# A gather stream spread over a second stage: the context's expert rows beside the main stream's first mixing

## The chip, the cores and the metric

The kernel runs on one core of one Trainium2 chip. The metric is the device time of one execution in microseconds (us), the median of three runs. Everything is in float32.

## The reference, cut to what matters

Two blocks run one after the other on 256 tokens of width 1024. The first has two layers of a hybrid mixer and a gated feed-forward. The second has two layers too, and a second input beside `x`, the context (256 tokens), which the second block alone uses:

```python
def reference(x, ..., ctx_2, ...):
    x = first_block(x, ...)                 # 2 x (state-space scan + retention + feed-forward)
    for l in range(2):                      # second_block
        h, hc = modulate(x, ...), modulate(ctx, ...)
        if l == 0: mix_c, kv_c = token_mix(hc)         # the context's own mixing
        else:      kv_c = keys_values(hc)
        mix_x = token_mix(h, kv_c)                     # the main stream's mixing
        x = x + m2 * mix_x
        x = x + m5 * peer(modulate(x), ...)            # experts
        if l == 0:
            ctx = ctx + m2c * mix_c
            ctx = ctx + m5c * peer(modulate(ctx), ...)
    return rmsnorm(x, final_g)

def peer(h):      # per token: 8 heads x 16 chosen experts = 128 rows of 1024
    act  = gate * gelu(sum(peer_down[e] * h))
    return sum_k act[k] * peer_up[e[k]]
```

The context's second state is read only by the keys and values of the second block's layer 1. So the context's experts are free to run anywhere between the context's own mixing and that point.

## The kernel before, in words

One program holds five engine programs. `Plan` writes one list of items (`put(kind, ...)`), and each engine walks through that list in order and does its share of each item. So the order of the list is the order of work on every engine, and an instruction that waits holds everything behind it on its engine.

Two generators write the list. `x_stream` is the main stream: the first block (two layers), then for l = 0 and 1 the mixing (`mix_phase`, with `mixer` inside) and the experts (`peer_x`). `context_stream` is the context: modulation, its mixing, and its experts (`peer_c`). `streams` interleaves them. Each `yield` adds a number of units to its stream's counter (7 where nothing is given), and the context gets a turn while its counter is at most `pace` times the main stream's. `("pace", p)` sets a new pace and aligns the counters, and `"alone"` writes all that is left of the context at once.

`PACES` is (0.8, 1.8, 1.1, 0.72): the last one is set when the context's routing is over and its expert rows begin. There are 512 such rows, in the order 128 `down` for the first 128 tokens, 128 `up` for them, then the same for the other 128 tokens. Each row is one indirect gather of 128 x 1024 floats (0.5 MB) issued by GpSimd (L2556), up to nine ahead in a ring of nine buffers, and one VectorE instruction: L2234 for `down` (multiply and reduce), L2245 for `up` (multiply and accumulate; it waits on the accumulate before it). Each row yields 1.5 units. The rows have no TensorE work. `peer_add` closes: SyncE loads a 0.5 MB row (L2627) once the last gathered row is read, and VectorE adds the result to the context (L2264, L2267).

In the list of the kernel before, the rows begin 1088 units before the end of the first block: 233 units of the feed-forward of layer 0 (22 `ffn_in`, 8 `ffn_out` and the last steps), 625 of layer 1's two mixers, and 230 of layer 1's feed-forward. The state-space scan is the first 248 units of those 625. At 0.72 they take 768 / 0.72 = 1067 units, so they end 20 units before the first block does, and `"alone"` finds nothing left.

The main stream's first mixing is 321 units: 34 for the normalisation, the low-rank projections and the keys and values, 28 for four steps of the query projection (`q_up`, with a rotation on VectorE at L2057 to L2061), 203 for attention with the gates, Fourier and pooling between its steps (`beside`), 28 for `mix` and 28 for `token_out`. An attention step gives VectorE a maximum (L2090), a scale, and, after ScalarE's exponential, a reciprocal (L2094); the transpose of that step on TensorE waits for the exponential. Of the 13 intervals between the third and the last of the 16 score steps, seven have one gate step (one weight chunk on TensorE) in between and six have none. All scratch of this mixing lies in the 27648 words from A0, except its twelve gate buffers (6144 words), which lie at B0 where the context has its memory, and which wait for the end of the context (`self.c_ok`).

Of the kernel before, what the change touches and what calls it, by code (L numbers as in the profile page):

```python
# [125 lines left out]
        self.before, self.ss, self.var, self.done = before, ss, var, done  # L126


PACES = (0.8, 1.8, 1.1, 0.72)
A_SIZE = 27648  # L130
BIG_N = 53208
SIDE = 8300
# [2 lines left out]
class Plan:  # L135
# [80 lines left out]
    def order(self):  # L216
# [7 lines left out]
        self.xmark = ar.at  # L224
        self.streams(self.x_stream(ar), self.context_stream(), PACES[0])
        self.put("finished", stored=(self.sem("d_out"), self.counts["d_out"]))
# [30 lines left out]

    def x_stream(self, ar):
        yield from self.first_block()
        yield "alone"  # L260
        for l in range(2):
            ar.at = self.xmark
            yield from self.mix_phase(self.px, Ring(self.wx), self.small, ar, l, self.X, 0, True)
            side = Arena(self.big, BIG_N - SIDE, SIDE)
            yield from self.peer_x(self.px, self.small, self.A0 + self.xmark, BIG_N - self.A0 - self.xmark - SIDE, l,
                                   self.X, iter(()) if l else self.context_keys(),
                                   [side.get(2048) for _ in range(3 if l else 4)], side if l else None)

    def context_stream(self):
# [5 lines left out]
        self.put("context_in")  # L275
        yield "pace", PACES[1]
        yield from self.mix_phase(self.pb, Ring(few), self.smallb, ar, 0, self.C, 1, False)
        yield "pace", PACES[2]
        yield from self.peer_c(self.pb, Ring(few), self.smallb, self.B0 + mark, BIG_N - self.B0 - mark, 9, 0, self.C)
# [592 lines left out]
    def mixer(self, banks, wr, sm, ar, l, hT, hT_ok, X, vec, rope_on, cs):  # L872
# [7 lines left out]
        wide = rope_on  # L880
# [3 lines left out]

        if early:
            zfT, AB, fT, zp, poT, pyT = mixed_buffers()
        if wide:
            far = ar if l else Arena(self.big, self.B0, BIG_N - self.B0)
            sg_slots = [Slot(far.get(512, (2, 256))) for _ in range(12)]
            for s in sg_slots:  # L890
                s.freed = self.c_ok
        mark = ar.at
        def spectral():
            w, u = self.load(wr, t["wzf"][l], 2048), banks.take()
            w.free(u.full)
            w2, ua = self.load(wr, t["dft"], 2048), [banks.take() for _ in range(2)]
            uf = banks.take()
            w2.free(uf.full)
            put("fourier", ws=[w, w2], u=u, ua=ua, uf=uf, hT=hT, zfT=zfT, AB=AB, fT=fT)
            got["f_ok"] = uf.free  # L900
            yield
            w, u = self.load(wr, t["wzp"][l], 2048), banks.take()
            w.free(u.full)
            w2, up = self.load(wr, t["pool"], 2048), banks.take()
            w2.free(up.full)
            w3, ug = self.load(wr, t["wgrp"][l], 256), banks.take()
            w3.free(ug.full)
            put("pool", ws=[w, w2, w3], u=u, up=up, ug=ug, hT=hT, zp=zp, poT=poT, pyT=pyT, psc=self.col[l, "psc"])
            got["py_ok"] = ug.free
            yield  # L910
# [34 lines left out]
        kv_ok = yield from kv  # L945
        if rope_on and l == 1:
            kv_ok += self.ctx_kv_ok
        low = self.low_turn(banks, sm, 256, cqn, cqT, self.col[l, "qg"], low["scaled"])
        put("low_turn_out", **low)
        turned = low["parts"][1].free  # L950
# [4 lines left out]
        for h in range(0, 8, 2):  # L955
            u = banks.take()
            q_ok = tick("q_turned") if rope_on else u.free
            put("q_up", ws=[w] if h == 0 else [], w_ok=w.full, wq=wq, cqT=cqT, Q=Q[:, h:h + 2, :], h=h, u=u, ready=turned,
                u2=banks.take() if rope_on else None, cs=cs, rt=rt, done=q_ok)
            yield  # L960
        w.free(u.full)

        nk = 4 if rope_on else 2

# [35 lines left out]
            yield from self.beside(fill, 11, attend(), 18)  # L1000
        else:
            yield from attend()
        if not wide or l == 0:
            ar.at = mark
        if not wide:
            if not early:
                zfT, AB, fT, zp, poT, pyT = mixed_buffers()
                yield from spectral()
            sg_slots = [Slot(ar.get(512, (2, 256))) for _ in range(3)]
# [34 lines left out]

    def routing(self, ar, b2, wr, sm, l, vec, hT, hT_ok, keys, keys_ok, iot, iot_ok, tvs, gat, eix, qts, GH):


        put, tick, t = self.put, self.tick, self.t
        SC0 = Ring([Slot(ar.get(256, (2, 128))) for _ in range(3 if GH == 8 else 8)])
        SC1 = ar.get(2048, (8, 256))  # L1050
# [18 lines left out]
        def gates(tt, g):  # L1069
            g3 = gat[:, tt, 16 * GH * g:16 * GH * g + 16 * GH].rearrange("p (h k) -> p h k", h=GH)  # L1070
            tv, c = tvs[tt][:, GH * g:GH * g + GH, :], sm[:, 32:32 + GH]
            exp = tick("gates_exp")
# [28 lines left out]
        def ranks(asking=None):  # L1101
            for tt in range(2):
                for h in range(8):
# [3 lines left out]
                    yield from rank(tt, h, by2(SC1[:, h, :]) if tt else sc.ap, ok, None if tt else sc)  # L1107
                    if (h + 1) % GH == 0:
                        yield from gates(tt, h // GH)

# [32 lines left out]
    def peer_c(self, banks, wr, sm, start, size, gslots, l, X):  # L1143

        put, tick, t = self.put, self.tick, self.t
        got = yield from self.peer_queries(banks, sm, start, size, l, X, 1, self.c_ok, 2)
        ar, mark, h2, act, gat, eix, gl, hT, hT_ok, keys, rest = got
        m3 = ar.at
        rows = self.modulated_rows(l, 1, 3, "norm2", h2, [ar.get(1024) for _ in range(3)], self.b_free)
        rows_ok = yield from rows(hT_ok)  # L1150
        ar.at = m3
        qts = Ring([Slot(ar.get(512, (2, 256)))])
        qts.slots[0].freed = rows_ok
        tvs = [ar.get(128, (8, 16)) for _ in range(2)]
        route, _, _, _, ix_ok, gates_ok, _ = self.routing(ar, banks, wr, sm, l, 1, hT, hT_ok, tvs=tvs, gat=gat, eix=eix, qts=qts,
                                                       GH=8, **rest)
        yield from route()
        yield "pace", PACES[3]
        ar.at = mark
        rr = Ring([Slot(ar.get(1024), self.sem(f"row{i}")) for i in range(gslots)])  # L1160
        steps = [(kind, tt, k) for tt in range(2) for kind in range(2) for k in range(128)]
        pending, ahead, nxt, act_ok = [], [], 0, {}
        acc_ok = {}
        for n, (kind, tt, k) in enumerate(steps):
            while nxt < len(steps) and len(ahead) < gslots:
                kind2, tt2, k2 = steps[nxt]
                s = rr.take()
                put("fetch", table=t["pboth"].rearrange("e (a d) -> (e a) d", a=2), s=s, index=eix[kind2][:, tt2, k2:k2 + 1],
                    ready=ix_ok[tt2][k2 // 16] if k2 % 16 == 0 else None, before=s.before or gates_ok[1, 0])
                ahead.append(s)  # L1170
                nxt += 1
            s = ahead.pop(0)
            done = tick("rows_read")
            s.free(done)
            if kind == 0:
                put("down", row=s.ap, full=s.full, h=h2[:, tt, :], out=act[:, tt, k:k + 1], done=done)
                if k == 127:
                    tanh = tick("gelu_tanh_c")
                    put("gelu_all", at=act[:, tt, :], u=gl, cubed=tick("gelu_cubed_c"), tanh=tanh)
                    act_ok[tt] = tick("act_done_c")  # L1180
                    put("gelu_all_end", at=act[:, tt, :], u=gl, gat=gat[:, tt, :], tanh=tanh, done=act_ok[tt])
            else:
                put("up", s=s, by=act[:, tt, k:k + 1], at=h2[:, tt, :], first=(k == 0), ready=act_ok[tt],
                    chain=acc_ok.get(tt), done=done)
                acc_ok[tt] = done
            yield 1.5
        end = tick("peer_added")
        put("peer_add", m5=rr.slots[0].ap, src=self.mods[l, 1, 5:6, :].to_broadcast([P, 1024]), loaded=tick("d_m5_c", 16),
            before=[done], acc=h2, X=X, done=end)
        self.c_ok, self.b_free = end, [end]  # L1190

    def peer_x(self, banks, sm, start, size, l, X, side, spare, last):
# [3 lines left out]
        wr = Ring(self.wx[:3])  # L1196
# [3 lines left out]
        ar, mark, h2, act, gat, eix, gl, hT, hT_ok, keys, rest = got  # L1200
        eix = eix[0]
        ag = ar.get(32)
        both = ar.get(1024)
        qts = Ring([Slot(both[:, 512 * i:512 * i + 512].rearrange("p (a n) -> p a n", a=2)) for i in range(2)])
        tvs = [ar.get(128, (8, 16)) for _ in range(2)]
        parts = self.routing(ar, Banks(banks.banks[4:6]), wr, sm, l, 0, hT, hT_ok, tvs=tvs, gat=gat, eix=[eix], qts=qts, GH=1, **rest)
        _, query, score, ranks, ix_ok, gates_ok, ended = parts
# [1 line left out]
        dgs = Ring([Slot(ar.get(128)) for _ in range(5)])  # L1209
        places = [ar.get(2048) for _ in range((ar.size - ar.at) // 2048)]  # L1210
        rows = self.modulated_rows(l, 0, 3, "norm2", h2, [places[-2][:, 0:1024], places[-2][:, 1024:2048], places[-1][:, 0:1024]],
                                   [self.x_ok])

        def ask():
            for i in range(8):
# [6 lines left out]
        route = ranks(asking)  # L1222
# [89 lines left out]
        for n, (tt, k) in enumerate(steps):  # L1312
            fetch_ahead()
            s, slot, _ = ahead.pop(0)
# [1482 lines left out]
```

## Time and profile before

| | |
|---|---|
| median of three runs | 4146.09 us (4141.56 to 4146.14) |
| span of the profiled execution | 4145.5 us |
| TensorE busy | 3651.7 us, 88% |
| VectorE busy | 2321.9 us, 56% |
| GpSimd busy | 1280.9 us, 31% |
| ScalarE busy | 657.1 us, 16% |
| mean granted TensorE clock | 0.955 |
| the context's 512 gathers | 1045.0 to 2131.1 us |
| the main stream's first mixing | 2182 to 2450 us |

Matmuls are pipelined and their ends are modelled, so a busy TensorE isn't one at its peak. The granted clock tells which part of full speed the array was given: 1.0 is the 2.4 GHz level, and a stretch that fell to the 1.2 GHz level for a part of its time shows a mean between 0.5 and 1.0.

### The profile page before, as it was taken

To read this page: it belongs to the slowest core of one execution; us is meant where nothing else is said; L and a number is where in the kernel's file an instruction comes from. 1 tells how busy PE (TensorE), PEld (TensorE's weight loads), DVE (VectorE), ACT (ScalarE), POOL (GpSimd) and SP (SyncE) were. 2 spreads that over 40 slices of the span, in tenths; PEclk is the share of its full clock that TensorE was granted. 3 is DMA by queue.
4 is the path that set the end of the run, shared out by engine and by line. 5 is a ranking of instruction groups with operands and counts; after the bars stand their busy time and mean duration, and the time that the engine had idled before them with its cause. 6 is when DMAs were issued, how large, how long until landed. Compare 5 with 4: busy or idle time off the path is not lost. (4 is left out here: it accounts for less than half of the span.)

```text
span 4145.5 us, 41044 instructions
## 1 busy us (share of the span) xinstructions
PE 3651.7 (88%) x14584; PEld 2584.5 (62%) x14584; DVE 2321.9 (56%) x5464; ACT 657.1 (16%) x1800; POOL 1280.9 (31%) x1125
## 2 busy tenths in 40 slices
PE   8988999999989889999988989778788898877777
PEld 6666788887756778888846875333335686433332
DVE  3432011457676897775762137787763226777875
ACT  2332101110001230000002211111112211111111
POOL 1100000000664566664540003445441002444442
PEclk9999999999999899999999999999999999998899
DMA  8742344334998889998973349999996227999997
GB/s 324 283 194 88 117 151 180 134 111 145 369 411 292 295 330 395 405 389 340 413 298 125 108 152 384 415 416 401 419 415 256 103 107 288 404 420 420 418 420 331
DMA packets 207818, 1208.65 MB, mean 292 GB/s; under 512 B 23696, under 2 KB 24848, under 8 KB 96000
## 3 DMA queue, kind: packets, MB, share of 16 engines
q0 software_dynamic: 154368, 855.71, 51.5%
q1 hardware_dynamic: 53248, 350.32, 22.2%
q8 instruction: 118, 1.93, 0.2%
q14 instruction: 84, 0.69, 0.0%
HBM read 1204.79 MB, written 1.15 MB: 291 GB/s over the span
## 5 line engine op out<-in xcount | busy, mean ns | idle before, releaser
L1363 PE MATMUL bank<-big 128*128 128x256 f32 (+5 forms) x9848 | 2148.4, 378 | 59.5 <-issue 8.7
L1363 PEld LDWEIGHTS bank<-big 128*128 128x128 f32 (+2 forms) x9848 | 1839.0, 192 | 374.3 <-issue 67.4
L2556 POOL DMA_INDIRECT big<-in_pboth,big x1024 | 1217.5, 1189 | 1210.0 <-PE bank L1750 695.2
L1750 PE MATMUL bank<-big 128*128 128x512 f32 x2048 | 984.3, 638 | 251.2 <-ACT big L2520 251.0
L2234 DVE CUSTOM_DVE_ANT_0 big<-big 128x1024 f32<-128x1024 f32 x768 | 928.0, 1224 | 347.1 <-DMA big<-in_pboth,big 343.0
L1750 PEld LDWEIGHTS bank<-big 128*128 128x128 f32 x2048 | 407.5, 204 | 816.6 <-issue 481.4
L2543 POOL TENSOR_TENSOR big<-big 128x1 f32<-128x1 f32 (+1 forms) x49 | 37.4, 763 | 1499.4 <-DVE big L1804 1499.4
L2245 DVE SCALAR_TENSOR_TENSOR big<-big 128x1024 f32<-128x1024 f32 x254 | 326.2, 1284 | 61.3 <-DMA big<-in_pboth,big 41.5
L2520 ACT ACTIVATE big<-big 128x128 f32<-128x128 f32 x512 | 165.1, 391 | 254.9 <-DVE big L2213 248.2
L1398 PE MATMUL bank<-big 128*128 128x128 f32 x596 | 93.0, 290 | 63.5 <-ACT big L2365 20.1
L2510 ACT ACTIVATE big<-big 128x4 f32<-128x4 f32 (+2 forms) x134 | 27.7, 207 | 742.3 <-DVE big L2209 742.2
L1553 PE MATMUL bank<-big 128*128 128x512 f32 x256 | 114.5, 609 | 23.4 <-DVE big L1968 23.4
L2090 DVE TENSOR_REDUCE big<-bank 128x1 f32<-128x512 f32 (+1 forms) x48 | 28.9, 602 | 175.0 <-PE bank L1651 174.1
L1398 PEld LDWEIGHTS bank<-big 128*128 128x128 f32 x596 | 72.9, 151 | 80.8 <-issue 35.2
L1877 DVE SCALAR_TENSOR_TENSOR big<-big,bank 128x512 f32<-128x512 f32 x32 | 22.0, 687 | 148.8 <-ACT big L2346 148.8
L1553 PEld LDWEIGHTS bank<-big 128*128 128x128 f32 x256 | 49.8, 195 | 87.2 <-issue 63.1
L1954 DVE SCALAR_TENSOR_TENSOR big<-big,bank 128x256 f32<-128x256 f32 x32 | 13.4, 420 | 153.4 <-PE bank L1363 153.3
L1861 DVE SCALAR_TENSOR_TENSOR big<-bank,big 128x255 f32<-128x255 f32 (+1 forms) x144 | 62.7, 477 | 60.0 <-ACT big L2334 58.3
L2303 ACT ACTIVATE big<-big 128x1024 f32<-128x1024 f32 x26 | 27.4, 1056 | 428.4 <-DVE big L1974 170.8
L2112 DVE SCALAR_TENSOR_TENSOR big<-big,bank 128x512 f32<-128x512 f32 x36 | 24.8, 688 | 103.6 <-PE bank L1363 103.6
L2488 ACT ACTIVATE big<-bank,big 128x256 f32<-128x256 f32 x72 | 30.3, 472 | 282.1 <-PE bank L1363 282.1
L2549 POOL DMA_DIRECT2D big<-in_wmod x48 | 25.9, 542 | 150.9 <-PE bank L1575 150.9
(203 smaller groups left out, 2177.4 us busy)
## 6 DMA issues: line engine op xcount, KB each, us to landing
big<-in_w SPq DMA_DIRECT2D x104, 1024.0 KB, 7.7
big<-in_wmod POOLq DMA_DIRECT2D x48, 1024.0 KB, 9.0
big<-in_wgu SPq DMA_DIRECT2D x44, 1024.0 KB, 8.1
big<-in_wzg SPq DMA_DIRECT2D x36, 1024.0 KB, 4.8
big<-in_wro SPq DMA_DIRECT2D x32, 1024.0 KB, 6.9
big<-in_wpq SPq DMA_DIRECT2D x24, 1024.0 KB, 6.0
big<-in_wd SPq DMA_DIRECT2D x22, 1024.0 KB, 8.4
big<-in_pboth,big POOLq DMA_INDIRECT x1024, 11.7
```

The costliest lines, as they stand in the source:

```text
L1363: last = pe.matmul(o, a, b, start=(i == 0), stop=(i == n - 1))
L1398: last = pe.transpose(o[:, i, :], b, ident)
L1553: last = pe.matmul(us[2 * tt + n].ap, act[:, 2 * i + k, tt * P:tt * P + P], wk[:, k, 512 * n:512 * n + 512], start=(i + k == 0), stop=False)
L1750: last = pe.matmul(u.ap, d.ap, row[:, 512 * i:512 * i + 512], start=(k == 0), stop=(k == 127))
L1861: i = v.scalar_tensor_tensor(c[:, m, s:256], o[:, m, 0:256 - s], conv["w"][m][:, 3 - s:4 - s], c[:, m, s:256], ALU.mult, ALU.add)
L2090: step(v.reduce_max(sm[:, c:c + 1], u.ap[:, 0:nk * P], AX.X))
L2234: v.tensor_tensor_reduce(row, row, h, 1.0, 0.0, ALU.mult, ALU.add, out).then_inc(done[0], 1)
L2245: v.scalar_tensor_tensor(at, s.ap, by, at, ALU.mult, ALU.add).then_inc(done[0], 1)
L2488: last = e.activation(sc.ap[:, m, :], by2(u.ap)[:, m, :], ACT.Tanh, scale=0.5, bias=bias[m])
L2520: s.activation(d.ap, p.ident, ACT.Copy, scale=by).then_inc(diag[0], 1)
L2543: g.tensor_tensor(r.sm[:, 8 + r.at:8 + r.at + r.n], r.sm[:, 4 + r.at:4 + r.at + r.n], r.sm[:, 12:13].to_broadcast([P, r.n]), ALU.pow).then ...
L2556: g.indirect_dma_start(out=s.ap, out_offset=None, in_=table, in_offset=bass.IndirectOffsetOnAxis(ap=index, axis=0)).then_inc(s.full[0], 16)
```

## The change

The context's rows get a lower pace (0.49) from their beginning, and the pace 0.72 again when the first block is over. `"alone"` moves from the end of the first block to the end of the first mixing (in layer 1 it finds nothing). Since the context's row buffers are then still in use beside the mixing, the mixing's gate buffers can't wait for the end of the context: eight of twelve move to the 4096 words of the context's two weight buffers, which are free once the context's last routing query is done (`few_ok`), and four lie over scratch of the same mixing, two over that of the keys and values and two over that of the query. The load of the rows' modulation in `peer_x` now waits for `c_ok` in layer 0.

```diff
-PACES = (0.8, 1.8, 1.1, 0.72)
+PACES = (0.8, 1.8, 1.1, 0.49, 0.72)
...
     def x_stream(self, ar):
         yield from self.first_block()
-        yield "alone"
+        yield "pace", PACES[4]
         for l in range(2):
             ar.at = self.xmark
             yield from self.mix_phase(self.px, Ring(self.wx), self.small, ar, l, self.X, 0, True)
+            yield "alone"
...
-        if wide:
-            far = ar if l else Arena(self.big, self.B0, BIG_N - self.B0)
-            sg_slots = [Slot(far.get(512, (2, 256))) for _ in range(12)]
+        if wide and l:
+            sg_slots = [Slot(ar.get(512, (2, 256))) for _ in range(12)]
             for s in sg_slots:
                 s.freed = self.c_ok
         mark = ar.at
+        if wide and not l:
+            far = Arena(self.big, self.B0, 4096)
+            sg_slots = [Slot(far.get(512, (2, 256))) for _ in range(8)]
+            for s in sg_slots:
+                s.freed = self.few_ok
+            sg_slots += [Slot(self.big[:, ar.start + mark + 512 * i:ar.start + mark + 512 * i + 512].rearrange("p (a b) -> p a b", a=2))
+                         for i in range(4)]
...
+        if wide and not l:
+            sg_slots[8].freed = sg_slots[9].freed = kv_ok[2]
...
+        if wide and not l:
+            sg_slots[10].freed = sg_slots[11].freed = q_ok
...
-        if not wide or l == 0:
+        if not wide:
             ar.at = mark
+        elif l == 0:
+            ar.at = mark + 2048
...
+        self.few_ok = ended["hT"]
         yield "pace", PACES[3]
...
-                                   [self.x_ok])
+                                   [self.x_ok] if l else [self.x_ok, self.c_ok])
```

## Rows read from the trace of the kernel before

**Rows 1.** The page: the costliest groups, the gathers' one.
```profile
L2556 POOL DMA_INDIRECT big<-in_pboth,big x1024 | 1217.5, 1189 | 1210.0 <-PE bank L1750 695.2
```

**Rows 2.** Windows from the rows' start: busy PE, PEld, DVE, ACT, POOL, PEclk, DMA, GB/s.
```profile
1054.00:1193.00 139.00, 126.83 (x576) 110.08 (x576) 101.25 (x183) 7.71 (x20) 90.12 (x73) 0.95 1.01 405
...
1271.00:1570.00 299.00, 251.07 (x1277) 219.95 (x1276) 255.94 (x392) 84.05 (x223) 169.27 (x133) 0.91 0.86 316
...
sum 1128.00, PE 1047.82 PEld 839.84 DVE 813.82 ACT 132.64 POOL 653.93; mean PE 149.69 PEld 119.98 DVE 116.26 ACT 18.95 POOL 93.42
```

**Rows 3.** The same view of the gathers alone, the state-space scan's stretch.
```profile
1271.00:1570.00 299.00, 164.88 (x128) 0.91 0.86 316
```

**Rows 4.** Waits of TensorE from 1030 to 2160 us: total, times, longest.
```profile
PE bank L1553 <- DVE big L1968: 23.4, 2, 12.3
PE bank L1398 <- ACT big L2365: 14.6, 3, 6.6
PE bank L1474 <- DVE big L1896: 13.0, 6, 3.3
...
PE bank L1363 <- DVE big L1861: 6.6, 2, 3.4
...
PE bank L1513 <- DVE big L1936: 2.8, 1, 2.8
```

**Rows 5.** Waits of VectorE in the same stretch.
```profile
DVE big L2234 <- DMA big<-in_pboth,big: 66.9, 49, 8.1
...
DVE big L2245 <- DMA big<-in_pboth,big: 41.5, 42, 2.2
```

**Rows 6.** Timeline of VectorE: three gathered rows in the scan, ten near the rows' end.
```profile
1425.29 4.12 DVE L2245 SCALAR_TENSOR_TENSOR big<-big 128x1024 f32<-128x1024 f32 x3
...
2129.58 14.06 DVE L2245 SCALAR_TENSOR_TENSOR big<-big 128x1024 f32<-128x1024 f32 x10 [2.20 <-DMA big<-in_pboth,big]
```

**Rows 7.** Windows of the first mixing: attention, and the sum of all stages.
```profile
2250.00:2390.00 140.00, 128.59 (x657) 109.45 (x658) 19.43 (x53) 35.94 (x86) 0.00 (x0) 0.97 0.28 98
...
sum 268.00, PE 245.34 PEld 203.92 DVE 54.11 ACT 52.53 POOL 1.95; mean PE 61.33 PEld 50.98 DVE 13.53 ACT 13.13 POOL 0.49
```

**Rows 8.** Timeline of VectorE: first and last of four query rotations.
```profile
2237.72 0.69 DVE L2057 TENSOR_TENSOR big<-bank,big 96x512 f32<-96x512 f32 x1 [9.66 <-PE bank L1644]
...
2249.84 0.69 DVE L2061 TENSOR_TENSOR big<-big 96x512 f32<-96x512 f32 x1
```

**Rows 9.** Timeline of VectorE in attention: the third step, three in the middle, the last.
```profile
2285.41 0.69 DVE L2090 TENSOR_REDUCE big<-bank 128x1 f32<-128x512 f32 x1 [1.45 <-PE bank L1651]
...
2335.72 0.69 DVE L2090 TENSOR_REDUCE big<-bank 128x1 f32<-128x512 f32 x1 [8.59 <-PE bank L1651]
...
2339.21 0.69 DVE L2090 TENSOR_REDUCE big<-bank 128x1 f32<-128x512 f32 x1 [1.55 <-PE bank L1651]
...
2341.00 0.16 DVE L2094 RECIPROCAL big<-big 128x1 f32<-128x1 f32 x1 [0.91 <-ACT big L2469]
2348.30 0.69 DVE L2090 TENSOR_REDUCE big<-bank 128x1 f32<-128x512 f32 x1 [7.13 <-PE bank L1651]
...
2373.45 0.69 DVE L2090 TENSOR_REDUCE big<-bank 128x1 f32<-128x512 f32 x1 [1.55 <-PE bank L1651]
```

**Rows 10.** Timeline around the context's last step in the kernel before.
```profile
2148.10 2.36 DVE L2264 TENSOR_TENSOR big<-big 128x1024 f32<-128x1024 f32 x2 [4.46 <-DMA big<-mods]
...
2150.50 2.36 DVE L2267 TENSOR_TENSOR big<-big 128x1024 f32<-128x1024 f32 x2
```

**Rows 11.** Timeline of VectorE at the end of the mixing, and TensorE in the routing after it.
```profile
2451.62 0.15 DVE L1804 TENSOR_SCALAR big<-big 128x1 f32<-128x1 f32 x1 [1.29 <-ACT big L2303]
...
2458.06 7.17 PE L1363 MATMUL bank<-big 128*128 128x256 f32 x32 [1.98 <-DVE big L2044]
...
2479.01 2.05 PE L1740 MATMUL bank<-big 128*128 128x128 f32 x8 [4.95 <-ACT big L2495]
```

More of the change, by code:

```diff
@@ L1154, in peer_c @@
         tvs = [ar.get(128, (8, 16)) for _ in range(2)]
-        route, _, _, _, ix_ok, gates_ok, _ = self.routing(ar, banks, wr, sm, l, 1, hT, hT_ok, tvs=tvs, gat=gat, eix=eix, qts=qts,
-                                                       GH=8, **rest)
+        route, _, _, _, ix_ok, gates_ok, ended = self.routing(ar, banks, wr, sm, l, 1, hT, hT_ok, tvs=tvs, gat=gat, eix=eix, qts=qts,
+                                                           GH=8, **rest)
         yield from route()
+        self.few_ok = ended["hT"]
         yield "pace", PACES[3]
```

## The prediction

> **What bounds the kernel now.** I read the windows by stage first, then the waits of TensorE, then the waits of VectorE, then the timeline at the places that these name.
>
> From the first gather to the end of the first block TensorE is busy 1047.8 of 1128 us [rows 2]: 80 us idle. Each stage's busy time times one minus its granted clock gives 40 us more that the low clock costs, 22.6 of them in the state-space scan (251.07 us at 0.91). So 120 us is all that any relief could give here. The reader is to see that the waits [rows 4] end on VectorE or on ScalarE behind it, none on a weight load. In the feed-forwards the gathers fill the DMA engines (share 1.01 at 405 GB/s [rows 2]) and VectorE waits 67 and 42 us for gathered rows [rows 5]. It falls behind, and TensorE finds the last activation of the feed-forward 11 to 12 us late, twice (23.4 us [rows 4]). In the scan the DMA isn't full (0.86), but VectorE is busy 256 of 299 us, and TensorE idles 48 us.
>
> The first mixing takes 268 us, with VectorE busy 54 and TensorE 245 [rows 7]. DMA and GpSimd are nearly free there. VectorE, however, is in the loop of attention: TensorE waits in each step for a maximum and an exponential [rows 9].
>
> **The change part by part.** The rows begin at the same place. 1088 units at 0.49, 1.5 a row, give 356 rows in the first block instead of 512. 156 are left. The mixing's 321 units at 0.72 take 155 of them, and one row and `peer_add` are left for "alone". 28 of the 156 are `down`, 128 `up`.
>
> *First block, scan.* 128 gathers fall into its 299 us [rows 3]. With 0.49/0.72 of them, 41 go. An `up` row costs VectorE 4.12/3 = 1.37 us [rows 6], so VectorE is relieved of 56 us and could be through in 243. TensorE's own floor is 251.07 x 0.91 = 228 us at full clock, and some 15 us of waits are left (the turn into the layer, the dt chain and the ends of the groups, of which rows cause only a part): 243 as well. Two engines with one floor don't both reach it. I take 254: **45 us saved**; bounds 20 (half of the three largest waits of the scan [rows 4], 34 us, and little clock) and 60.
>
> *First block, feed-forwards.* A chunk of weights is 1 MB and 32 matmuls, 126.83 x 32 / 576 = 7.05 us [rows 2], so the weights need 149 GB/s. With 7 x 0.49 / 1.5 = 2.29 rows of 0.5 MB in that time the rows need 170: 319 together, under the 405 that is seen. So VectorE no longer waits for rows, and behind the last chunk it has at most two or three of them. I keep 2 us of each 11 to 12: 19 saved, with 3 for the clock after the gap: **22 us**; bounds 12 and 24. The wait of 2.8 us in the retention also goes: **3 us**. Sum of the gain **70 us**, bounds 35 and 95 (120 less 25 for turns between layers that no row causes).
>
> *Mixing, first steps.* Some four rows now stand on VectorE between the final norm of the first block and the mixing's statistics, then one or two before each of three short steps of the normalisation, which TensorE waits for. `down` rows are instructions of about 1.2 us. Counted along the chain: **6 us** (3 to 9). The powers on GpSimd stand behind fetches of 1.19 us [rows 1]; I have put 1 us of the 6 for that.
>
> *Query projection.* VectorE's four rotations take 2237.7 to 2250.5, 12.8 us [rows 8], 2.1 of work each. Between two of them come 7 x 0.72 / 1.5 = 3.36 rows, 4.5 us. The last ends 3 x 6.6 + 2.1 = 21.9 us after the first begins, and the first score step waits for it: **9 us**.
>
> *Attention.* From one maximum to the next it is 3.5 us without a gate and 9.1 with one [rows 9]. VectorE holds itself for 1.95 us in each (maximum to the end of the reciprocal). With 3.36 rows behind every step, at 1.41 with the gap to the next instruction, 4.74 us are added. Over the 13 intervals from the third score step to the last there are 20 steps: 20 x 4.74 + 13 x 2.1 = 122 us, where 88 stand now (2285.4 to 2373.5 [rows 9]): 34 us. Before that only one gap, behind the pooling, has no cover: 3 us. **37 us**; below, 15 (VectorE's idle time, 120.6 of 140 us [rows 7], against 97 rows x 1.41 = 137 us, so 16 at least); above, 50.
>
> *Mix steps.* VectorE has five instructions over 128x512 in each, 0.69 as in [rows 9], with 0.6 between them: 4.1 us + 4.74, where TensorE needs 7.05: **7 us** over four. `token_out` has two of them, 1.4 + 4.7, less than TensorE's 7: nothing.
>
> *The end.* After the last `token_out` five rows (7 us), then the load that SyncE issues only now (4.46 us) and the four additions (4.8 us [rows 10]): 16.3 us, where the next statistics now follow 1.3 us behind [rows 11]: **15 us**. Before, the same step lay under the feed-forward at no cost. Behind that load in SyncE's queue stand three weight chunks of the routing. They are needed 8 us behind the mixing's end now [rows 11], about 23 then: covered.
>
> *The moved buffers.* The eight at B0 were free long ago, two wait for the values and two for the query, and the gates that use those four come at the end of attention. Nothing; if I am wrong, one gate step, 7 us. The new wait for `c_ok` on SyncE stands behind the end of the context in any case: nothing.
>
> Sum of the loss 6 + 9 + 37 + 7 + 15 = 74, with **3** for TensorE's clock in the gaps: **77 us**; bounds 46 and 95. Against the gain of 70 that is **+7 us**. The profiled span is 4145.5 us, which is within 0.6 us of the median: **4152 us**.
>
> On the price of a row: the trace has ten `up` rows in 14.06 us, 1.28 of work each and 0.13 of the wait for the accumulate before, and three in 4.12 [rows 6]. The Trainium skill (VectorE: DVE Perf Modes, The DRAIN you can't avoid) has it that a semaphore after each instruction costs nothing over one after the last. By the page the 97 rows of attention would cost 12 us less than by the row; the row decides.
>
> **The rivals.**
>
> *The mixing hides the rows* (faster). For: DMA share 0.28 and VectorE idle 86% there [rows 7], and TensorE is busy 92%, so nothing is asked of the bound engine. If TensorE's gate steps cover the rows, the query projection and attention cost 12 instead of 46, and the time is 4152 - 34 = 4118. Against: the list is walked in order, and the sum of VectorE alone exceeds the stretch. It decides when these two cost under 30 us.
>
> *The clock* (slower). In the scan TensorE has idle gaps of up to 6.6 us [rows 4] and a mean clock of 0.91 [rows 2], and in the routing 8 matmuls took 2.05 us after a gap of 4.95 [rows 11]. If attention falls from 0.97 to 0.85, since its gaps would come more often than the scan's, and TensorE becomes the bound beside VectorE, its 128.6 us of work take 18 more: 4170. The Trainium skill (TensorE: Matmul & The Clock Gate, HAM oscillation) describes just that: bursts of matmuls with repeated waits between them start each burst at half speed. The trace agrees in the scan; in the mixing no run shows it yet.
>
> *The first block keeps its waits* (slower). Group ends in the scan wait for a chain of ScalarE, GpSimd and ScalarE (14.6 us [rows 4]) that may not be the rows'. If the scan gives 15 and not 45, the time is 4182.
>
> **How the numbers follow.** A measurement here can tell 0.2% from no change: 4138 to 4154. As worked: 0.42, with a range of its own from 4138 to 4168 (of it 0.06 faster, 0.22 same, 0.14 slower). Hidden: 0.25 (0.22 faster, 0.03 same). Clock: 0.15. Waits kept: 0.18. So faster 0.28, same 0.25, slower 0.47. The range 4116 to 4184 takes in the times of all four and leaves out what lies beyond the second's and the last's.
>
> **What would show it.** Gathers run on to the end of the mixing, about 340 us after its start instead of 268. The scan's stretch is 254 us, VectorE's share in it under 85%, and the DMA share in the feed-forwards near 0.8, with 2 us before `ffn_out`. In attention TensorE waits for the maximum behind rows, 6.8 us a step without gate, and 11.6 with one. The first statistics of the experts come 16 us behind the last `token_out`. The forecast is wrong if attention isn't lengthened by 25 us or more, or if the first block ends less than 50 or more than 90 us earlier.

## The result, and the profile after

| | kernel before | changed kernel |
|---|---|---|
| median, run side by side | 4144.33 us | 4151.75 us |
| span of the profiled execution | 4145.5 us | 4151.3 us |
| mean granted TensorE clock | 0.955 | 0.952 |

The ratio is 1.0018 (95% interval 1.0011 to 1.0024): slower by 0.18%. The interval leaves out 1, so the difference is real, but it is less than the 0.2% that the prediction had set as what can be told from no change. In the changed kernel most lines have moved by 14 (L1553 is L1567, L2245 is L2259).

The two traces are best laid beside each other at marks that both have. The last column is how much earlier the changed kernel is, and its steps are the terms of the sum.

| mark (start, us) | before | after | ahead |
|---|---|---|---|
| layer 0, `ffn_out` | 1193.40 | 1183.10 | 10.3 |
| first matmuls after that feed-forward | 1274.27 | 1261.77 | 12.5 |
| end of the scan (the turn of its last group) | 1567.88 | 1517.25 | 50.6 |
| layer 1, `ffn_out` | 2098.87 | 2032.57 | 66.3 |
| end of the first block (first matmuls after it) | 2176.45 | 2108.41 | 68.0 |
| mixing, first projection | 2188.59 | 2127.49 | 61.1 |
| first maximum of attention | 2252.78 | 2201.78 | 51.0 |
| third maximum | 2285.41 | 2235.12 | 50.3 |
| last maximum | 2373.45 | 2351.92 | 21.5 |
| `token_out` | 2420.81 | 2406.88 | 13.9 |
| first routing chunk of the experts | 2458.06 | 2462.20 | -4.1 |
| end of the span | 4145.5 | 4151.3 | -5.8 |

So 68.0 us were won in the first block and 73.8 given back, 54 of them in the first mixing up to `token_out`, 18 at its end and 1.7 behind the first routing chunk.

**Where they were won.** TensorE's waits from 1030 to 2110 us in the changed kernel (total, times, longest), beside [rows 4]:

```profile
PE bank L1412 <- ACT big L2379: 6.4, 2, 4.3
...
PE bank L1567 <- DVE big L1982: 3.3, 2, 1.6
PE bank L1377 <- DVE big L1875: 2.6, 2, 2.2
PE bank L1488 <- DVE big L1910: 2.5, 2, 1.9
```

The two waits before `ffn_out` fell from 23.4 to 3.3 us; the three largest of the scan fell from 34.2 to 11.5. By windows (the stages as in [rows 2], then the first mixing; busy PE, PEld, DVE, ACT, POOL, PEclk, DMA share, GB/s):

```profile
1054.00:1183.00 129.00, 126.76 (x576) 110.08 (x576) 73.20 (x141) 7.68 (x20) 62.93 (x52) 0.98 0.96 358
1259.00:1521.00 262.00, 241.25 (x1288) 212.78 (x1286) 205.38 (x387) 84.08 (x223) 118.20 (x94) 0.97 0.79 278
2114.00:2410.00 296.00, 232.10 (x1056) 190.60 (x1057) 225.40 (x285) 52.76 (x124) 184.15 (x145) 0.87 0.93 350
```

In the scan the clock rose from 0.91 to 0.97 and VectorE's share fell from 86% to 78%. In the mixing VectorE went from 54 us to 225, and the clock is 0.87.

**Where they were given back.** VectorE in attention, two steps with a gate in between and one without:

```profile
2287.71 0.69 DVE L2104 TENSOR_REDUCE big<-bank 128x1 f32<-128x512 f32 x1
2288.43 0.15 DVE L2106 TENSOR_SCALAR big<-big 128x1 f32<-128x1 f32 x1
2289.49 0.16 DVE L2108 RECIPROCAL big<-big 128x1 f32<-128x1 f32 x1 [0.91 <-ACT big L2483]
2289.60 9.80 DVE L2259 SCALAR_TENSOR_TENSOR big<-big 128x1024 f32<-128x1024 f32 x7
2299.32 0.69 DVE L2104 TENSOR_REDUCE big<-bank 128x1 f32<-128x512 f32 x1
...
2301.21 4.12 DVE L2259 SCALAR_TENSOR_TENSOR big<-big 128x1024 f32<-128x1024 f32 x3
2305.25 0.68 DVE L2104 TENSOR_REDUCE big<-bank 128x1 f32<-128x512 f32 x1
...
2307.13 9.80 DVE L2259 SCALAR_TENSOR_TENSOR big<-big 128x1024 f32<-128x1024 f32 x7
```

In [rows 9] each maximum has "<-PE" behind it, with up to 8.6 us of idle time. Here, from the third to the last, none has: the gathered rows end and the maximum begins. The scores lay ready, and TensorE is now the one that waits. The only idle time of VectorE left is 0.91 us for the exponential, which no row fills, because the rows stand behind the reciprocal in the list. From one maximum to the next it is 11.61 us with seven rows and 5.93 with three.

The end of the mixing, VectorE and TensorE in order of time:

```profile
2436.16 3.62 PE L1422 MATMUL bank<-big 128*128 128x256 f32 x16
...
2437.82 6.96 DVE L2259 SCALAR_TENSOR_TENSOR big<-big 128x1024 f32<-128x1024 f32 x5
...
2449.48 2.36 DVE L2278 TENSOR_TENSOR big<-big 128x1024 f32<-128x1024 f32 x2 [4.71 <-DMA big<-mods]
2451.88 2.36 DVE L2281 TENSOR_TENSOR big<-big 128x1024 f32<-128x1024 f32 x2
2454.28 0.15 DVE L1818 TENSOR_SCALAR big<-big 128x1 f32<-128x1 f32 x1
...
2455.14 2.08 PE L1422 MATMUL bank<-big 128*128 128x256 f32 x4 [15.36 <-POOL big L2557]
```

Five rows, 4.71 us for a load, four additions, and only then the first statistics of the experts; TensorE stands 15.36 us. Its next four matmuls take 0.52 us each, the 16 before the gap 0.23: the 1.2 and the 2.4 GHz level.

### The profile page after: what moved, and what is told of

Same layout as the page of the kernel before. It is cut to its first block and busy times, and to the rows that moved or that the text cites. A ratio compares the mean times of both kernels' runs of the same rounds, so it can differ in the third digit from the quotient of the medians.

```text
span 4151.3 us, 41049 instructions
## 1 busy us (share of the span) xinstructions
PE 3655.0 (88%) x14584; PEld 2586.9 (62%) x14584; DVE 2319.2 (56%) x5464; ACT 656.9 (16%) x1800; POOL 1292.8 (31%) x1125
## 3 DMA queue, kind: packets, MB, share of 16 engines
HBM read 1204.79 MB, written 1.15 MB: 290 GB/s over the span
## 5 line engine op out<-in xcount | busy, mean ns | idle before, releaser
L2259 DVE SCALAR_TENSOR_TENSOR big<-big 128x1024 f32<-128x1024 f32 x254 | 326.6, 1286 | 25.6 <-DMA big<-in_pboth,big 1.3
L1891 DVE SCALAR_TENSOR_TENSOR big<-big,bank 128x512 f32<-128x512 f32 x32 | 22.1, 689 | 178.8 <-ACT big L2360 178.8
L1968 DVE SCALAR_TENSOR_TENSOR big<-big,bank 128x256 f32<-128x256 f32 x32 | 13.5, 421 | 179.4 <-PE bank L1377 179.3
L1567 PE MATMUL bank<-big 128*128 128x512 f32 x256 | 110.6, 593 | 3.3 <-DVE big L1982 3.3
L1567 PEld LDWEIGHTS bank<-big 128*128 128x128 f32 x256 | 48.3, 189 | 64.7 <-issue 60.6
L1980 DVE SCALAR_TENSOR_TENSOR big<-big,bank 128x256 f32<-128x256 f32 x44 | 18.5, 421 | 123.7 <-ACT big L2419 117.5
L2104 DVE TENSOR_REDUCE big<-bank 128x1 f32<-128x512 f32 (+1 forms) x48 | 28.8, 600 | 103.9 <-PE bank L1665 103.0
L1422 PE MATMUL bank<-big 128*128 128x256 f32 x160 | 44.1, 436 | 35.1 <-POOL big L2557 17.7
```

The lines of the kernel that those rows point to most:

```text
L1422: pe.matmul(u.ap[:, 0:256], ident, p.masks, start=True, stop=True)
L1567: last = pe.matmul(us[2 * tt + n].ap, act[:, 2 * i + k, tt * P:tt * P + P], wk[:, k, 512 * n:512 * n + 512], start=(i + k == 0), stop=False)
L2259: v.scalar_tensor_tensor(at, s.ap, by, at, ALU.mult, ALU.add).then_inc(done[0], 1)
```

## The experiments

The kernel before ran again beside each group of kernels; its medians were 4142.1 to 4145.12 us. Ratios are to it.

**Buffers alone.** Everything of the change except the pace, so that all 512 rows stay in the first block.

```diff
-PACES = (0.8, 1.8, 1.1, 0.49, 0.72)
+PACES = (0.8, 1.8, 1.1, 0.72, 0.72)
```

> Only the moved gate buffers, their waits and the moved end mark are kept; the row pace is 0.72 throughout, so all rows again end inside the first block. Theory (the buffers cost nothing, the price lies in the rows on VectorE's queue): the time of the kernel before, 4144 us, give or take 3. Rival (a gate step waits for its borrowed scratch): 4148 to 4151.

4141.28 us, ratio 0.9998 (0.9989 to 1.0008). The moved gate buffers, the wait for `c_ok` and the later mark cost nothing.

**The gain alone.** The changed kernel without the rows that would fall into the mixing: 156 rows and the closing addition to the context are left out of the computation.

```diff
+        steps = steps[:356]
...
-        put("peer_add", ...)
+        end = done
```

> The changed kernel without the last 156 of the context's 512 rows and without the addition that closes its experts: the part that would run beside the mixing is left out. Theory: the first block ends 68 us earlier and nothing is paid for it, 4144 - 68 = 4076 us, give or take 4, so the price of the 156 rows in the mixing is 4152 - 4076 = 76, against 77 worked out. Rival (the mixing hides most of the rows and the first block gives less than its trace shows): well above, 4100 to 4120.

4074.93 us, ratio 0.9841 (0.9822 to 0.9861). The first block's relief is worth 68.0 us by itself (4142.92 - 4074.93). What the 156 rows and the addition cost in the mixing is 4151.75 - 4074.93 = 77 us, or 75 if each median is taken against the kernel before that ran beside it (68.0 + 7.4); the marks give 73.8. Both halves of the sum are measured apart.

**The end alone.** The closing addition no longer stands at the end of the mixing, but 60 units behind it, in the second experts' stage. The mixing's pace is 0.73 instead of 0.72.

```diff
-            yield "alone"
...
+        yield 60
         end = tick("peer_added")
```

> The changed kernel with the closing addition of the context's experts moved behind the normalisation of the main stream's experts, where VectorE waits for the first scores; 0.73 instead of 0.72, so that the last row stays in the mixing. Theory (five rows, the 4.7 us load and 4.8 us of additions stand on the path at the mixing's end): 9 to 10 us less than the changed kernel, 4142 us, since the five rows before the statistics stay. Rival (something else would hold the experts' start): 4152.

4141.13 us, ratio 0.9998 (0.9989 to 1.0008): 10.6 us less than the changed kernel by the medians, 9 if each is taken against the kernel before beside it. VectorE at the end of the mixing in this kernel:

```profile
2440.08 4.12 DVE L2259 SCALAR_TENSOR_TENSOR big<-big 128x1024 f32<-128x1024 f32 x3
2444.12 0.14 DVE L1818 TENSOR_SCALAR big<-big 128x1 f32<-128x1 f32 x1
...
2450.36 2.35 DVE L2278 TENSOR_TENSOR big<-big 128x1024 f32<-128x1024 f32 x2
```

The statistics follow straight behind the rows, and the addition comes 6 us later where TensorE doesn't need VectorE. The wait for the load is gone as well. With 0.73 three rows are left behind the last `token_out` where the changed kernel has five, so some 3 us of the difference are two rows that moved, and not the addition.

**VectorE's load or the gathers' bytes?** Two kernels made from the kernel before tell the two causes in the first block apart. In the first, each VectorE instruction of a context row handles 512 of its 1024 columns (half of every row's product and sum is left out); the gathers stay whole.

```diff
-                put("down", row=s.ap, full=s.full, h=h2[:, tt, :], ...)
+                put("down", row=s.ap[:, 0:512], full=s.full, h=h2[:, tt, 0:512], ...)
...
-            v.scalar_tensor_tensor(at, s.ap, by, at, ALU.mult, ALU.add)...
+            v.scalar_tensor_tensor(at[:, 0:512], s.ap[:, 0:512], by, at[:, 0:512], ALU.mult, ALU.add)...
```

> The kernel before, with VectorE's instruction of each of the context's rows over 512 of its 1024 columns (the other half is left out), and the gathers whole. It asks what the first block's 68 us come from. Theory (in the scan VectorE's time, in the feed-forwards late gathers): the scan gives 35 to 45 us, the 20 us of the feed-forwards stay, 4143 - 42 = 4101. Rival (contention of the transfers throughout): 4125 or more.

In the second each gather brings 512 columns, which VectorE reads twice, so that its work stays as long (the second half of each row is replaced by the first, and a `down` row waits for the row before it).

```diff
-                put("fetch", table=t["pboth"].rearrange("e (a d) -> (e a) d", a=2), ...)
+                put("fetch", table=t["pboth"].rearrange("e (a d) -> (e a) d", a=4), ...)
...
-            v.scalar_tensor_tensor(at, s.ap, by, at, ALU.mult, ALU.add)...
+            v.scalar_tensor_tensor(by2(at), s.ap.unsqueeze(1).to_broadcast([P, 2, 512]), by, by2(at), ...)
```

> The kernel before, with each of the context's gathers over 512 columns instead of 1024 (the values are those of other rows), VectorE's work as long as before: it reads the half row twice, and a down row waits for the one before it. Theory: the feed-forwards give their 20 us and the scan gives nothing or loses a little, 4143 - 22 = 4121. Rival (contention of the transfers throughout): 4090 or less.

Half the VectorE work: 4095.94 us, ratio 0.9883 (0.9865 to 0.9901). Half the bytes: 4120.3 us, ratio 0.9944 (0.9926 to 0.9962). For half the VectorE work, the scan's window:

```profile
1264.00:1522.00 258.00, 239.23 (x1258) 210.78 (x1258) 187.91 (x388) 82.12 (x220) 141.27 (x130) 0.95 0.94 355
```

and TensorE's waits in the first block:

```profile
PE bank L1553 <- DVE big L1968: 16.7, 2, 9.9
PE bank L1398 <- ACT big L2365: 10.8, 3, 5.0
```

For half the bytes, the same two views (its lines are one or more further down):

```profile
1258.00:1553.00 295.00, 248.01 (x1258) 217.52 (x1258) 253.33 (x387) 81.72 (x220) 164.07 (x130) 0.92 0.61 203
```

```profile
PE bank L1399 <- ACT big L2371: 13.0, 3, 6.6
PE bank L1475 <- DVE big L1897: 11.6, 5, 3.3
...
PE bank L1554 <- DVE big L1969: 3.6, 2, 1.9
```

By the marks of the table the scan takes 293.6 us before (1274.27 to 1567.88), 258.3 with half the VectorE work and 295.2 with half the bytes. So the scan was held by VectorE's time: half of it gives 35.3 us, half the bytes give nothing. The waits before `ffn_out`, 23.4 us before, are 3.6 with half the bytes and 16.7 with half the work.

The feed-forwards are less clean. Half the bytes give 25.6 us outside the scan (16.0 up to its start, 9.6 behind its end), half the VectorE work still gives 16.3 (10.1 and 6.2), although the DMA engines stay full there (share 1.02 at 413 GB/s up to the first `ffn_out`). The expectation had those 20 us stay with half the work, and was 5 us too high in sum. The late gathers weigh more, but VectorE's own work is a second cause of the same wait, and the two amounts can't be added. The lower pace relieves both, which is why one number in `PACES` gives gains in both kinds of stage.

**The clock.** Filler matmuls after each score step of attention, so that TensorE doesn't stand while it waits for the exponential.

```diff
     def att_turnp(p, nk, u, ready, **_):
         opened(u)
+        if nk == 4:
+            keep_busy(u, 8)
         pe.wait_ge(*ready)
```

> The changed kernel with eight matmuls more on TensorE before each wait for an exponential in the attention of the second block (both layers), so that its clock doesn't fall in the gaps that the rows make. Theory (VectorE's queue sets the pace of attention, the low clock lies under it): the time of the changed kernel, 4152, give or take 4. Rival (the clock of 0.87 in the mixing is a good part of the price): 4142 or less.

4214.89 us, ratio 1.017 (1.0153 to 1.0187): neither theory's number. The line is also reached in layer 1's attention, where VectorE has no rows and TensorE had no time to spare: from its first maximum to its last 163.9 us instead of 118.4, 45.5 of the 63 lost. But in layer 0 the run tells what was asked. From the third maximum to the last (changed kernel first, filler second):

```profile
2235.00:2352.00 117.00, 93.71 (x432) 80.37 (x433) 97.57 (x108) 27.52 (x67) 83.85 (x68) 0.82 0.97 373
```

```profile
2239.00:2364.00 125.00, 124.17 (x647) 108.93 (x646) 98.14 (x108) 27.66 (x67) 83.91 (x68) 1.00 0.94 347
```

and two maxima of the kernel with the filler:

```profile
2287.99 0.69 DVE L2106 TENSOR_REDUCE big<-bank 128x1 f32<-128x512 f32 x1 [0.88 <-PE bank L1665]
...
2293.93 0.68 DVE L2106 TENSOR_REDUCE big<-bank 128x1 f32<-128x512 f32 x1
```

The clock went from 0.82 to 1.00, and a step without a gate takes 5.94 us against 5.93: TensorE's clock didn't set it. (The steps with a gate grew because the filler filled TensorE there.) For the steps with a gate the changed kernel's own trace answers: their scores lay ready too. So there the low clock of attention lies under VectorE's rows.

**Fewer rows in the mixing.** Pace 0.56 in the first block and 0.5 in the mixing: 408 rows and 104, where the change has 356 and 156. The last `up` rows then stand before the last `token_out`.

```diff
-PACES = (0.8, 1.8, 1.1, 0.49, 0.72)
+PACES = (0.8, 1.8, 1.1, 0.56, 0.5)
```

> Paces 0.56 and 0.50 instead of 0.49 and 0.72: 408 rows in the first block, 104 in the mixing, the closing addition between the last two steps of the mixing. Theory (the price arises only where VectorE's rows outlast TensorE's step): intervals with a gate cost nothing, those without 1.9 us each; price 5 for the start, 5 for the query, 11 for attention, 1 for the mix steps, 3 for the end, 25; the first block gives 54; 4144 - 54 + 25 = 4115 us. Rival (the price goes with the number of rows, 72 x 104 / 156 = 48): 4138.

4117.8 us, ratio 0.9942 (0.9923 to 0.9962). The matmuls after the first block begin at 2126.85 us, so of its 68 us 49.6 are kept; the first routing chunk begins at 2429.21, 28.9 ahead of [rows 11]. The price up to there falls from 72.1 us to 20.7. In attention, two intervals:

```profile
2278.07 0.68 DVE L2104 TENSOR_REDUCE big<-bank 128x1 f32<-128x512 f32 x1
...
2279.95 5.54 DVE L2259 SCALAR_TENSOR_TENSOR big<-big 128x1024 f32<-128x1024 f32 x4
2286.45 0.69 DVE L2104 TENSOR_REDUCE big<-bank 128x1 f32<-128x512 f32 x1 [0.95 <-PE bank L1665]
...
2288.34 4.12 DVE L2259 SCALAR_TENSOR_TENSOR big<-big 128x1024 f32<-128x1024 f32 x3
2292.38 0.68 DVE L2104 TENSOR_REDUCE big<-bank 128x1 f32<-128x512 f32 x1
```

Four rows (5.54 us) fit under a gate, and VectorE waits 0.95 us for TensorE again. From the third maximum to the last it is 91.2 us, where [rows 9] have 88.0: attention costs 3 us instead of 29. The addition still stands behind VectorE's part of the last `token_out` (2414.84 us) and ahead of the statistics:

```profile
2416.49 2.36 DVE L2278 TENSOR_TENSOR big<-big 128x1024 f32<-128x1024 f32 x2 [0.23 <-DMA big<-mods]
```

**A quiet start.** Pace 0.56 in the first block again, but with no rows until attention begins (pace 0), and 0.62 from there; then the same with 0.6 and the addition 60 units behind the mixing.

```diff
-PACES = (0.8, 1.8, 1.1, 0.49, 0.72)
+PACES = (0.8, 1.8, 1.1, 0.56, 0.0, 0.62)
...
         if wide:
+            if not l:
+                yield "pace", PACES[5]
             yield from self.beside(fill, 11, attend(), 18)
```

> Pace 0.56 in the first block, none in the mixing up to attention, 0.62 from there: 408 rows in the first block, one before attention, 103 from attention on. Theory (in e4_split the rows among the short dependent steps before attention cost 12 us, while attention with gates has room): 10 us less for the start, 3 more in attention, 4118 - 7 = 4111. Rival (the start's price only moves into attention): 4118 or more.

> As e6_quiet with 0.60, and the closing addition of the context behind the normalisation of the main stream's experts. Theory: the 5 us that e4_split still pays at the mixing's end go too, 4106 us. Rival (the addition holds the first ranking instead): 4111.

4137.51 us (ratio 0.9984, 0.9975 to 0.9994) and 4123.06 (0.9948, 0.9931 to 0.9964): 27 and 17 us over what was expected, both worse than the split alone. Of the first, TensorE's waits of the mixing:

```profile
PE bank L1379 <- DMA big<-in_wout: 11.2, 1, 11.2
PE bank L1414 <- DVE big L2053: 5.9, 1, 5.9
```

The first line is new: a chunk of weights is late by 11.2 us. With the addition late it is gone. The second shows that the quiet start wasn't quiet: it is the 5.4 us wait of the changed kernel. Five rows (6.95 us from 2129.58) still stand between the block's final norm and the mixing's statistics, ahead of the new pace in the list. First maximum and last are at 2205.02 and 2344.60 us, and with pace 0.5 throughout at 2215.08 and 2340.30: 10 us are won ahead of attention and 14 lost in it, since the same rows are pressed into fewer steps: the rival had the price move into attention, and it did.

**The late chunk.** Still fewer rows in the mixing (437 and 75), once with the addition where the list puts it, between two `mix` steps, and once 60 units behind the mixing. The third kernel is the 0.56 and 0.5 of before with the late addition.

```diff
-PACES = (0.8, 1.8, 1.1, 0.49, 0.72)
+PACES = (0.8, 1.8, 1.1, 0.6, 0.42)
```

> Still fewer rows in the mixing: pace 0.6 in the first block and 0.42 in the mixing, 437 rows and 75. From the runs so far: 156 rows fewer in the first block bring 68 us, 104 fewer bring 50, so the rows nearest to the old pace bring most, 0.48 us each, and the last 52 bring 0.35. By 0.48 a row, 75 rows bring 36 us. In the mixing 104 rows cost 21 us. If that price falls with the rows (0.2 each), 75 cost 15: 4144 - 36 + 15 = 4123 us. If with two rows and fewer behind a step the price is nearly gone and only some 4 us of the first steps are left, it is 4112 us.

> The pace 0.6 and 0.42 again (437 rows and 75), with the closing addition 60 units behind the mixing. With the addition between the mix steps, TensorE waited 9.9 us there for a chunk of weights. If that chunk's load stood in SyncE's queue behind the load of the addition, which waits for the last gathered row, the wait goes and the 8 to 10 us come back: 4115 us. If the chunk is late because the gathers and the weights share the DMA engines, the wait stays: 4123 us.

> The even split of the earlier run (pace 0.56 in the first block, 0.5 in the mixing: 408 rows and 104), with the closing addition not ahead of the last token_out but 60 units behind the mixing, where the second experts' normalisation stands. The split left a price of 5 us between the last token_out and the first routing chunk. If that is the addition and its load, they go under the query of the second experts: 4113 us. If it is only the later arrival of the stream's rows and TensorE's clock behind the wait, nothing changes: 4118 us.

| | median | ratio (interval) |
|---|---|---|
| 437 and 75, addition between the `mix` steps | 4123.75 | 0.9961 (0.9949 to 0.9974) |
| 437 and 75, addition late | 4111.1 | 0.992 (0.9906 to 0.9934) |
| 408 and 104, addition late | 4113.84 | 0.9934 (0.9917 to 0.995) |

SyncE's queue in the first of them, and TensorE:

```profile
2361.30 0.33 SPq L2641 DMA_DIRECT2D big<-mods  x1
2361.67 1.55 SPq L2588 DMA_DIRECT2D big<-in_woabc  x3
...
2368.28 22.73 PE L1377 MATMUL bank<-big 128*128 128x256 f32 x96 [9.88 <-DMA big<-in_woabc]
```

SyncE issues the addition's load at 2361.30, when the last gathered row has been read (VectorE's last one began at 2359.99). Right behind it, in 1.55 us, go three chunks of weights, which need no row and had stood in the queue; with the addition late all four of these chunks are out by 2342.5. TensorE gets the first 9.88 us late. With the addition late:

```profile
2353.04 28.00 PE L1377 MATMUL bank<-big 128*128 128x256 f32 x128 [0.68 <-ACT big L2471]
2382.65 28.00 PE L1377 MATMUL bank<-big 128*128 128x256 f32 x128 [1.60 <-DVE big L2131]
```

All 128 `mix` matmuls run without a gap, and the time is 12.7 us lower. So it was the queue, not a full DMA. The 4123.75 us of the 437 and 75 split with the addition between the `mix` steps met the first of its two expected numbers (4123), but not for the reason given there: 9.88 us of it are this chunk, and without it the other number (4112) is the nearer. For 408 and 104 rows the late addition brings 4.0 us by the medians, whose intervals overlap; the traces are clearer, 37.2 us from the first `token_out` matmul to the first routing chunk where the addition in its old place took 42.4. 437 and 75 rows with the late addition is the fastest kernel of the study, 33 us under the kernel before and some 41 under the changed one.

## Why the prediction was right, point by point

It named 4152 us by 70 won and 77 lost; it is 4151.75 by 68.0 and 73.8. The mechanism is the forecast one, but that the total came within 1 us is in part luck: the scan was put 7 us too high and the feed-forwards 5 too low, attention 7.5 too high and the end 3 too low, and single runs of the changed kernel spread from 4145.38 to 4159.54.

- *Scan*: 45 forecast, 38.1 measured (50.6 - 12.5). The stretch took 255.5 us, 254 forecast. The end point was right; the start was a window of 299 us, and from mark to mark the scan took 293.6. That the cause is VectorE's time is shown by the run with half the work: 258 us.
- *Feed-forwards and retention*: 22 and 3 forecast. 12.5 up to the end of the first one, 17.4 from the scan's end to the block's: 29.9. The last activation is waited for 1.64 us, not 2. The text gave this gain to late gathers; the run with half the bytes bears that out for the most part (25.6 us), the run with half the VectorE work (16.3 us) shows the second cause that it left out. The forecast rate was too low: 358 GB/s and a DMA share of 0.96, where the text had 319 and 0.8; the relief came although the DMA engines stayed nearly full.
- *First steps*: 6, measured 6.9. *Query projection*: 9, measured 10.1, of which the rotations have 7.1 (2176.59 to 2196.46 us against 12.8). The other 3.1 lie behind the last rotation, where the turn from `down` to `up` (five small instructions for the gates, 2197.76 to 2199.64) and three rows stand ahead of the first maximum; the sum had no term for that turn.
- *Attention*: 37, measured 0.7 + 28.8 = 29.5. The rows were counted right: in the 13 intervals there are 67, for which 20 x 3.36 had been reckoned. The two kinds of interval give their price, (11.61 - 5.93) / 4 = 1.42 us a row, and leave 5.93 - 3 x 1.42 = 1.67 us for VectorE's own part, where the sum had 2.1: 13 x 0.43 = 5.6 us too much. That the rows are issued in order behind the reciprocal is the mechanism, as forecast. The Trainium skill (VectorE: DVE Perf Modes, The DRAIN you can't avoid) says that a semaphore after each instruction adds nothing. No run here leaves the semaphores out, so that sentence isn't tested. What the trace has is that `up` rows, each waiting for the accumulate before, come every 1.42 us for 1.28 of work, and `down` rows, which wait for no row, every 1.15 for 1.22; the price by the row held.
- *Mix steps*: 7, measured 7.6. *The end*: 15, measured 18.0. From the last `token_out` on VectorE to the second statistics it takes 15.2 longer; 1.4 lie ahead of that, and 1.5 behind it, where TensorE starts at the 1.2 GHz level after its gap (four matmuls in 2.08 us against 1.13 in the kernel before). The *clock* had 3: these 1.4 and 1.5 are the size of it, and they are inside the 18.0. The 1.7 us behind the first routing chunk weren't traced to anything.
- *Buffers and the wait for `c_ok`*: nothing, measured nothing (0.9998).
- *The forecast signs*: the last gather was issued at 2427.8 us, 319 after the block's end, where 340 was said. A step without a gate takes 5.93 us and not 6.8, and the DMA share in the feed-forward is 0.96 and not 0.8. These held: 11.6 us a step with a gate, a scan of 255.5 us, VectorE's share in it under 85%, 1.64 us before `ffn_out` for 2, and statistics 16 us behind the last `token_out` (2437.09 to 2454.28: 17).
- *The routing's chunks behind the load*: called covered, and they were. The first routing chunk waits 1.58 us for VectorE and for no load. It is the same order in SyncE's queue that cost 9.88 us where the addition stood between two `mix` steps.

The rivals. *The mixing hides the rows* fell at this load: query projection and attention cost 40 us, and it decided under 30. At two thirds of the load it is true: first projection to last maximum takes 194.7 us (2145.60 to 2340.30) against 184.9 before, so there they cost 10. *The clock*: its first half came true (attention fell to 0.82), its second didn't, since raising the clock to 1.00 shortened no step. The Trainium skill (TensorE: Matmul & The Clock Gate, HAM oscillation) has bursts of matmuls with repeated waits start at half speed; the trace agrees, but here that time lay under VectorE's rows except for the start behind the 15.36 us gap. *The first block keeps its waits* fell: 38 us in the scan and not 15.

The gain in the first block isn't even: by the first matmuls after the block it is 68.0 us at 356 rows, 49.6 at 408 and 47.0 at 437 (2129.44 instead of 2176.45; two runs of one pace differ by up to 2 us). The traces show where it goes. From mark to mark the scan takes 293.6 us at pace 0.72, 275.9 at 0.6, 270.0 at 0.56 and 255.5 at 0.49, while the feed-forwards and the retention keep 29.3, 26.0 and 29.9 us of gain at the three lower paces. So the feed-forwards have all their relief at 0.6 already, and of the 18.4 us between 408 and 356 rows 14.5 are the scan's.

What stays open: the 1 to 5 us that each split loses behind its first routing chunk. Nor was a kernel tried that has no rows between the end of the block and the mixing's first projection, where 7 us lie in the changed kernel and as many in the 408 and 104 split.

## What to carry to other kernels

Work put beside a stage is free only where the engine's own chain leaves room behind each step: count rows per step against the other engine's time for that step, not idle shares over the stage (VectorE was idle for 86% of attention, and putting 156 rows into the mixing cost 72 us; two thirds of them cost 21). When a stream is spread over two stages, try the split itself as a size, because both curves bend: here the feed-forwards gave all they had at the first step down, the scan went on giving, and attention charged only for the rows that outlast TensorE's step. And place the stream's last item, with its load, where nothing in the same queue is urgent: that was worth some 10 and 13 us in two pairs of kernels, and 4, not clear of noise, in a third.

## What the runs showed of the hardware

- One load that waited for VectorE held weight loads that waited for nothing, 9.88 and 11.2 us long. TensorE's waits name a DMA of weights there, and only SyncE's timeline shows that the cause was the order of the queue.
- A chain of `up` rows costs 1.42 us each at 1.28 of work. Three take 4.12 us beside a TensorE with a mean clock of 0.82, and the same in the scan before [rows 6] at 0.91.
- At 358 GB/s the first feed-forward waited 1.64 us for its last activation, at 384 GB/s (408 rows, DMA share 0.99) again 1.64, and at 405 GB/s [rows 2] 12.3 (share 1.01). The shares look alike, and only the waits tell them apart.
